# The two softmax attentions' small products over 64 or 32 rows of their own, instead of zero-padded 128 rows

## What is computed

```python
def fox_attention(q, k, v, log_f):            # q, k: 4 heads x 512 x 64
    c = jnp.cumsum(log_f, axis=-1)
    ...
        logits = jnp.einsum('bhqd,bhkd->bhqk', qi, k) * scale + ci[..., :, None] - c[:, :, None, :]
        logits = jnp.where(pos_k[None, :] <= pos_q[:, None], logits, -jnp.inf)
        probs = jax.nn.softmax(logits, axis=-1)
        return jnp.einsum('bhqk,bhkd->bhqd', probs, v)

def causal_block_attention(q_nope, q_pe, k_nope, k_pe, v):   # 8 heads
    ...
        sc = (jnp.einsum('bqhd,bkhd->bhqk', qn_b, k_nope)    # over 128
              + jnp.einsum('bqhr,bkr->bhqk', qr_b, k_pe))    # over 64, one k_pe for all heads
        ...
        p = jax.nn.softmax(jnp.where(mask, sc, neg), axis=-1).astype(v.dtype)
        return jnp.einsum('bhqk,bhkd->bqhd', p, v)
```

## Time and profile before

| | us |
|---|---|
| median of 3 runs | 1900.09 |
| lowest and highest of them | 1898.42, 1900.93 |
| the profiled execution, its own time | 1897.2 |
| its span, first to last instruction | 1895.4 |
| mean granted clock of TensorE, as a share of 2.4 GHz | 0.989 |

### The profile page before, as it was taken

The page is one execution under the profiler, slowest core; times in us unless marked ns, Lnnn a source line. Parts: engine busy times, 40 slices in busy tenths (PEclk is TensorE's granted clock), DMA queues, the critical chain, the costliest instruction groups (busy, mean ns, idle before and its releaser), DMA issues.

```text
span 1895.4 us, 27507 instructions
## 1 busy us (share of the span) xinstructions
PE 1850.9 (98%) x10095; PEld 1498.7 (79%) x10095; DVE 932.3 (49%) x1309; ACT 729.5 (38%) x1067; POOL 214.4 (11%) x180
## 2 busy tenths in 40 slices
PE   8999899899999999999999999999999999999998
PEld 6787678587888888888888888888776778888886
DVE  6453576646776743355544344333667353443322
ACT  6535433545444432322342323233555342332222
POOL 0030011021111110000111111101000211111110
PEclk9999988999999999999999999999999999999999
DMA  6302100123333333333333333333330233333332
GB/s 188 89 25 57 45 24 23 67 76 92 98 90 100 97 92 99 101 93 97 100 90 99 100 94 94 92 101 97 85 92 1 66 91 100 90 99 97 92 97 70
DMA packets 309228, 160.97 MB, mean 85 GB/s; under 512 B 12688, under 2 KB 306832, under 8 KB 309024
## 3 DMA queue, kind: packets, MB, share of 16 engines
q1 hardware_dynamic: 308080, 157.21, 28.7%
q0 software_dynamic: 640, 2.17, 0.3%
q10 hardware_dynamic: 432, 0.52, 0.1%
HBM read 157.79 MB, written 2.10 MB: 84 GB/s over the span
## 4 chain that ended last, share of the span: by engine, by line
PE 93%; DVE 3%; ACT 2%; issue 1%; POOL 0%; DMA 0%; ACTq 0%; DVEq 0%; POOLq 0%
PE ps L372 27%; PE ps L374 27%; PE ps L373 27%; PE ps L1723 1%; PE ps L1471 1%; PE ps L1181 1%; PE ps L1481 1%; PE ps L2019 1%; PE ps L2020 1%; PE ps L1714 1%; PE ps L922 1%; PE ps L1092 1%; PE ps L1435 0%; DVE xlo L446 0%; ACT whi L359 0%
## 5 line engine op out<-in xcount | busy, mean ns | idle before, releaser
L372 PE MATMUL ps<-xhi,whi 128*128 128x512 f32 x1656 | 656.4, 396 | 3.4 <-DVE wlo L367 2.3
L373 PE MATMUL ps<-xlo,whi 128*128 128x512 f32 x1656 | 647.3, 391 | 0.0
L374 PE MATMUL ps<-xhi,wlo 128*128 128x512 f32 x1656 | 647.1, 391 | 0.0
L359 ACT ACTIVATE whi<-raw 128x1024 fp32r<-128x1024 f32 (+2 forms) x297 | 309.0, 1040 | 707.6 <-PE ps L374 707.1
L367 DVE TENSOR_TENSOR wlo<-raw,whi 128x1024 fp32r<-128x1024 f32 (+2 forms) x297 | 364.9, 1229 | 280.4 <-ACT whi L359 280.4
L372 PEld LDWEIGHTS ps<-xhi,whi 128*128 128x128 f32 x1656 | 312.6, 189 | 73.4 <-issue 5.8
L373 PEld LDWEIGHTS ps<-xlo,whi 128*128 128x128 f32 x1656 | 312.6, 189 | 65.9 <-issue 2.4
L374 PEld LDWEIGHTS ps<-xhi,wlo 128*128 128x128 f32 x1656 | 312.4, 189 | 65.4
L622 DVE TENSOR_TENSOR zS<-ps,rs 128x512 f32<-128x512 f32 x132 | 91.3, 691 | 296.9 <-PE ps L374 284.8
L374 PE MATMUL ps<-h_hi,wlo 128*128 128x512 f32 x528 | 205.4, 389 | 0.0
L372 PE MATMUL ps<-h_hi,whi 128*128 128x512 f32 x528 | 205.4, 389 | 0.0
(11 more groups left out here) (334 smaller groups left out, 1568.1 us busy)
## 6 DMA issues: line engine op xcount, KB each, us to landing
raw<-in_conv_ffn_w SPq DMA_DIRECT2D x52, 512.0 KB, 3.8
raw<-in_mla_ffn_w SPq DMA_DIRECT2D x52, 512.0 KB, 3.8
raw<-in_w_up SPq DMA_DIRECT2D x44, 512.0 KB, 3.8
raw<-in_w_in SPq DMA_DIRECT2D x28, 512.0 KB, 3.8
raw<-in_conv_w_in SPq DMA_DIRECT2D x24, 512.0 KB, 3.8
raw<-in_w_down SPq DMA_DIRECT2D x16, 448.0 KB, 3.7
raw<-in_conv_ffn_w SPq DMA_DIRECT2D x16, 448.0 KB, 3.7
raw<-in_mla_ffn_w SPq DMA_DIRECT2D x16, 448.0 KB, 3.8
```

The lines of the kernel that those rows point to most:

```text
L359: a.activation(whi[:, u % PARTS, 0:n], raw[:, u % RAW, 0:n], ACT.Copy).then_inc(hi_split, 1)
L372: t_.matmul(out, wh, xh, start=first, stop=False)
L373: t_.matmul(out, wh, xl, start=False, stop=False)
L374: return t_.matmul(out, wl, xh, start=False, stop=last)
```

## The change

Each of the small products now contracts over the rows that hold data: the logits of a `fox` head over its own 64 rows (`HEAD_ROWS[h % 2]`) of queries and keys, its gate row over 32 rows (`FOX_GATES`: rows 0 to 31 for even heads, 96 to 127 for odd ones), and the rotated part of an `mla` head over its 64 rows. The masked key copies with `pool_fox`, the clearing in `pool_mla` and the waits for them go away. For the odd heads, VectorE copies the gate sums of rows 0 to 3 to rows 96 to 99 of `grow` after `dve_gcol`, and the constants of heads 1 and 3 have their 1 in rows 97 and 99. `kpz` keeps one tile that holds the key twice.

```diff
--- before.py
+++ after.py
@@ -84,7 +84,7 @@
     put("perm", (s // 64 == r // 64) & (s % 64 == (r + 32) % 64))
     put("near", (i[:, None] // LC == np.arange(HC * 8)[None, :] // HC) & (i[:, None] % LC < HC))
     for h in range(4):
-        put(f"foxrow{h}", (s == h) & (r >= 0))
+        put(f"foxrow{h}", (s == h + 96 * (h % 2)) & (r >= 0))
     for p in range(2):
         put(f"beta{p}", s == 32 + 2 * p + r // DH)
         put(f"gpair{p}", s == 64 + 2 * p + r // DH)
@@ -995,6 +995,7 @@
                     dst = gate_cols[64 * hh:64 * hh + 64].rearrange("p q v (t two) -> p t q v two", two=2)[:, :, :, :, odd]
                     v.tensor_copy(dst, bank[64 * odd:64 * odd + 64, :, 1:4, hh:hh + 3:2]).then_inc(
                         *step("dve", "gcol taken" if hh and odd else f"gcol {hh} {odd}"))
+            v.tensor_copy(grow[96:100, :], grow[0:4, :]).then_inc(*step("dve", "fox gates again"))
 
         def act_ecol(act):
             act.wait_ge(*after("gcol taken"))
@@ -1778,7 +1779,8 @@
             each(heads - 1)
 
 
-        FZ, FVT, FO = (2, 3, 14, 15), 12, 10
+        FVT, FO = 12, 10
+        FOX_GATES = (slice(0, 32), slice(96, P))
         FOX_IN = [mx[:, 0, :], mx[:, 1, :], mx[:, 6, :], mx[:, 7, :], mixT[:, 0, :], mixT[:, 1, :]]
         PB["fox"] = mx[:, 16:20, :]
         fox_PT = wtile(20, 8).rearrange("p (b k t) -> p b k t", b=2, t=T)
@@ -1803,7 +1805,9 @@
 
         def pe_fox(pe):
             def ready(pe, h):
-                pe.wait_ge(*after(f"fox kz{h}"))
+                pe.wait_ge(*after(f"fox qk {2 + h // 2}"))
+                if h == 1:
+                    pe.wait_ge(*after("fox gates again"))
                 pe.wait_ge(*after(f"fox v{h // 2} taken"))
                 if X_AGAIN[h]:
                     pe_x_again(pe, X_AGAIN[h])
@@ -1813,8 +1817,10 @@
                 W = P * (i + 1)
                 if (h, i) == (0, 2):
                     pe_head_norm(pe, "hg out", range(2))
-                t_.matmul(out, FOX_QK[h // 2][:, i * P:(i + 1) * P], mx[:, FZ[h], 0:W], start=True, stop=False)
-                return t_.matmul(out, C(f"foxrow{h}"), grow[:, 0:W], start=False, stop=True)
+                rows, gate = HEAD_ROWS[h % 2], FOX_GATES[h % 2]
+                t_.matmul(out, FOX_QK[h // 2][rows, i * P:(i + 1) * P], FOX_QK[2 + h // 2][rows, 0:W], start=True,
+                          stop=False)
+                return t_.matmul(out, C(f"foxrow{h}")[gate, :], grow[gate, 0:W], start=False, stop=True)
 
             attn_pe(pe, "fox", 4, logits, lambda k, h: mx[:, FVT + h // 2, k * P:(k + 1) * P], fox_PT, ready)
             pe_x_again(pe, X_AGAIN[4])
@@ -1859,15 +1865,6 @@
                 dve.wait_ge(*after(f"fox out rs{i}"))
                 v.scalar_tensor_tensor(mixT[:, i, :], FOX_O[i], par("fox_on_g"), hr[i], ALU.mult,
                                        ALU.mult).then_inc(*step("dve", f"mix{i}"))
-
-        def pool_fox(pool):
-            for h in range(4):
-                pool.wait_ge(*after(f"fox qk {2 + h // 2}"))
-                if h == 1:
-                    pool.wait_ge(*after("hg1 intra5 0 full"))
-                g.tensor_scalar(mx[:, FZ[h], :], FOX_QK[2 + h // 2], C("hmask")[:, h % 2:h % 2 + 1], None,
-                                ALU.mult).then_inc(*step("pool", f"fox kz{h}"))
-
 
         MIX_ORDER = (2, 3, 6, 7, 4, 5, 0, 1)
 
@@ -2017,7 +2014,8 @@
                 blk = slice(i * P, (i + 1) * P)
                 W = P * (i + 1)
                 t_.matmul(out, qn[:, h, blk], kn[:, h, 0:W], start=True, stop=False)
-                return t_.matmul(out, qp[:, h // 2, blk], kpz[:, h % 2, 0:W], start=False, stop=True)
+                rows = HEAD_ROWS[h % 2]
+                return t_.matmul(out, qp[rows, h // 2, blk], kpz[rows, 0, 0:W], start=False, stop=True)
 
             attn_pe(pe, "mla", NH2, logits, lambda k, h: vtok[:, k, h * P:(h + 1) * P], mla_PT, ready)
 
@@ -2081,10 +2079,6 @@
                 a.activation(xhi[:, h, :], full(act, f"mla O{h}"), ACT.Copy).then_inc(*step("act", f"mla hi{h}"))
             attn_act(act, "mla", NH2, mla_PT, each)
 
-        def pool_mla(pool):
-            pool.wait_ge(x_lo, XPART0["mla_norm_g_2"])
-            g.memset(kpz[:, :, :], 0.0).then_inc(*step("pool", "kpz zeros"))
-
         def act_positions(act):
             act.dma_start(turns[:, :], A["positions_2"][0].partition_broadcast(P)).then_inc(pos_loaded, 16)
 
@@ -2173,9 +2167,8 @@
                             dve_rotate(dve, f"q swapped{i}", qp[:, i, :], f"rotated{i}",
                                        f"rotated{i - 1}" if i else "k rotated")
                 if gr == 0:
-                    dve.wait_ge(*after("kpz zeros"))
                     for half in range(2):
-                        v.tensor_copy(kpz[64 * half:64 * half + 64, half, :], kraw[64:P, :]).then_inc(
+                        v.tensor_copy(kpz[64 * half:64 * half + 64, 0, :], kraw[64:P, :]).then_inc(
                             *step("dve", f"kpz{half}"))
 
             def each(h):
@@ -2276,7 +2269,6 @@
                         pool_gdn_triangle(pool, p)
             for nm in LA:
                 pool_la_setup(pool, nm)
-            pool_fox(pool)
             pool_load_again(pool)
             pool_residual(pool, "w_out", "mix1")
             pool_products(pool, "ffn1_up", FT, h_hi, h_lo)
@@ -2285,7 +2277,6 @@
             pool_residual(pool, "conv_out", "conv norm sum full")
             pool_products(pool, "ffn2_up", FT, h_hi, h_lo)
             pool_residual(pool, "ffn2_down", "ffn2 norm sum full")
-            pool_mla(pool)
             pool_residual(pool, "w_o", "mla norm sum full")
             pool_products(pool, "ffn3_up", FT, h3_hi, h3_lo)
             pool_residual(pool, "ffn3_down", "ffn3 norm sum full")
```

## The result

| | before | after |
|---|---|---|
| median of 4 runs each, us | 1900.51 | 1928.49 |
| lowest and highest, us | 1898.42, 1901.01 | 1927.67, 1929.81 |
| profiled execution, us | 1897.2 | 1928.59 |
| mean granted clock of TensorE in it | 0.989 | 0.978 |

The account below looks back on a forecast made before the run. TensorE, 93% of the chain's 1895.4 us span, was taken to bound the kernel. Changes of rows in `mla` (11.6 us) and `fox` (5.7) plus the copy (0.4) made 17.7 us: 1917.5 us forecast, range 1912 to 1922.5.

Parts of the forecast that it names:

- `mla`, 11.6 us: Second attention: two changes of rows in each of 32 tiles, 12.5 us, less 0.9 hidden in head 0.
- The 0.195: Price in us taken for each change of row count on TensorE, in either direction; the rows gave 0.14 to 0.20.
- the likeliest error: The forecast errs most if a change costs differently before the many narrow transposes than before the wide products measured.
- 64 to 32 rows within the same 64: `fox`, logits to gate product: taken at 0.195 us a change; the rival that it is free, 1915.6 us, had chance 0.17.
- `fox`, 5.7 us for changes: First attention: 29 of 48 changes of rows counted on the chain, at 0.195 us each.
- The choice of 29: `fox` changes taken as on TensorE's chain; the other 19 fall where VectorE or ScalarE carries it.
- The copy, 0.41 us: Added VectorE copy at the gate columns, while TensorE waits for the low part: 0.41 us, all on the chain.
- The rival of the other side: Small products run beside each other, gate beside logits in `fox`: 1893.8 us, faster; chance 0.03.
- The clock term: Open term on the 3.5 us half-clock fall in `fox`: -1.75 us if it vanishes, 0 if elsewhere, +1.75 for each more.
- the rival with more falls: The clock falls one to three further times, 1.75 to 5.3 us more, 1919 to 1923 us; chance 0.06.
- The -1.75 us: Gain if the one half-clock fall in `fox` vanishes: half of its 3.5 us.

Follow-up runs that it names:

- e4: Kernel before plus, in each `fox` tile, two one-column 32-row products with zero stationary operand (64 changes of rows in all): 1910.02 us, ratio 1.0060.
- e9: Kernel with only the `fox` part of the change, plus a 128-row, 256-column product, later overwritten, ahead of each tile's logits: 1910.69 us, against 1920.35 without it.
- e10: Kernel before with five input-projection pieces spread two, two, one among the linear attentions' 16-column products: 1902.27 us, ratio 1.0013.
- e1: Kernel before with the `mla` edits alone, `fox` as before: 1909.91 us, ratio 1.0060.
- e7: Kernel before with only the added VectorE copy of four gate rows, which nothing reads: 1900.21 us, ratio 1.0002.
- e3: Kernel with only the `fox` part of the change, its gate product over the logits' 64 rows instead of 32: 1911.01 us, ratio 1.0057 to before.
- e5: Kernel before with `fox` logits over the head's own 64 rows and the gate product still over 128: 1907.64 us, ratio 1.0043.
- e8: Kernel before with masked 128-row `fox` logits kept and only the gate product cut to 32 rows: 1910.01 us, ratio 1.0054.
- e11: Kernel before with five input-projection pieces spread one by one among the linear attentions' 16-column products: 1911.87 us, ratio 1.0059.

## Why the prediction was wrong

**The direction and its mechanism were right.** A change of the number of rows costs TensorE time, in either direction, and TensorE bounds both stages.

**`mla`, 11.6 us: over-sized, 8.95 measured.** The 0.195 holds for the change into the 64-row product (0.19) but not for the one out of it, into 128-column transposes (0.15). I had named that as the likeliest error. With 0.34 per tile, 32 x 0.34 = 10.9, less what TensorE's old waits took up (0.9 by its idle time, and the 0.11 of each head). The head came to 8.96 us, where I had 9.25.

**64 to 32 rows within the same 64: right not to take it as free.** In the rows above the 64-row pair of 384 columns ends at 373.51 + 0.91 = 374.42 and the 32-row pair behind it at 374.35 + 0.92 = 375.27. That is 0.85 us from end to end, against 0.65 for such a pair in a steady stream: 0.20 for the change from 64 to 32, about the 0.195 taken. The rule quoted from the Trainium skill, "TensorEngine Tiling (Array Packing)", Key Properties, agrees.

**`fox`, 5.7 us for changes: about right for what it counted.** 6.8 by e4's price, 4.9 by the account of busy time; the two don't agree better than that. The total is 46 changes and not 48 (two pairs of tiles share one), so 110 in the kernel and not 112. The choice of 29 lost its basis, since at the lower clock TensorE carries the chain nearly throughout.

**The copy, 0.41 us: right in the trace** (0.42, and 0.45 more wait), too small to see in a median.

**The rival of the other side** didn't come about: the logits' and gate products follow each other in every row shown, none starts with its partner.

**The clock term failed, and with it the forecast.** The step reads: "With the changes TensorE has more to do in that stretch, and the fall may vanish (-1.75) or come elsewhere (0)." I took it that the clock follows how much TensorE is busy, and the rival with more falls, at 0.06, was sized at one to three of the length seen before. What the runs showed in its place: 37.6 us more at the lower level, with TensorE busy for all but 1.0 us of it, worth 18.3 us of its time and, with the waits that this filled, some 12.6 us of the stage (19.4 - 6.8). e9 shows that too little full-row work is the cause, e4 that the changes are not. The -1.75 us for a fall that vanishes was too much as well: in e10, whose `fox` has no fall, the stage took 46.24 us, against 46.4 to 47.0 in before, e1 and e7, with the same `fox` and one fall of 3.4 us.

The Trainium skill, "TensorE: Matmul & The Clock Gate", Part 1, says that the gate goes by "how busy the PE has been recently", with idle gaps as what to avoid. The row of 375.10 to 388.80, busy 13.70 of 13.70 us at 0.50, does not agree if busy is what a profile calls busy; the measurement decides. The falls in `fox` of before, e3, e5 and e8, each behind a stretch with 1.1 to 1.6 of 3.40 us busy, do agree.

**What stays open.** Why `mla`, with 64-row products in every tile, keeps the full clock: its other product has 128 rows, a mean of 96, but e5 with the same mean in its small products had 13.7 us low. Its transposes and output products are those of `fox`, so they don't tell the two apart. What fits is that e5's fall began behind a stretch of waits, busy 1.42 of 3.40 us, and TensorE waits for only 1.2 of the 73 us in `mla`; this was not tested. What in the narrow products of the linear attentions takes the clock down, their few columns, few rows or frequent changes, is open too, and so is why pieces two at a time shortened the falls and single ones doubled them. A gate product in the other half of the rows, which might have run beside the logits' one, was not tried, as two products at once in one bank.

## What to carry to other kernels

Cutting a float32 product's contraction from 128 rows to 64 or 32 saves no TensorE time if it isn't run beside another, costs 0.15 to 0.20 us at each change of row count, and can halve the clock for most of a stage (41 of 66 us here); zeros in the unused rows were the cheaper choice by 28 us here. When an edit leaves TensorE fewer rows at work, price the clock as a term of its own, at worst the stage's TensorE time once more, and look for the granted clock in the stretches before believing any sum of lengths. Look, too, at what TensorE did before the clock fell: behind a wait, the products decided here how long the fall lasted (3.4 or 13.7 to 20.5 us); with TensorE busy throughout, as in after, it is a question of what the products are, not of what they wait for.

## What the runs showed of the hardware that was not expected

- TensorE at 1.2 GHz while busy 13.70 of 13.70 us, in a stretch of 64-, 32- and 128-row float32 products.
- Adding 6.9 us of full-row products made the kernel 9.7 us faster (e9).
- 64 changes of row count with one-column products between full-row ones left the clock as it was (3.4 us low in `fox`), at 0.22 us of TensorE's time each (e4).
- Falls that begin behind a wait lasted 3.4 us before full-row products and 13.7 to 20.5 us before products of fewer rows (before; e5, e3, e8).
- Full-row products spread singly among 16-column products didn't hold the clock up, but were slowed with them (e11: 47.8 us low where before had 23.9); two at a time they shortened the falls (e10: 17.1).
